# Block-diagonal 128x128 operands for the batched triangular inverses of an RWKV-7 recurrence: three engines share the masking anew

## The reference, cut to what matters

```python
def step(S, inp):
    r_t, w_t, k_t, v_t, kk_t, kka_t = inp
    sa = jnp.einsum('bhvk,bhk->bhv', S, kk_t)
    S = (S * w_t[:, :, None, :]
         - sa[..., None] * kka_t[:, :, None, :]
         + v_t[..., None] * k_t[:, :, None, :])
    y_t = jnp.einsum('bhvk,bhk->bhv', S, r_t)
    return S, y_t
```

## Time and profile before

| what | value |
|---|---|
| time, median of 3 runs | 2113.97 us (2113.3 to 2117.39) |
| the profiled execution | 2113.75 us, of which the span is 2112.0 us |
| mean granted TensorE clock | 0.992 |
| busy: TensorE, VectorE, ScalarE, GpSimd | 95%, 67%, 48%, 8% of the span |
| recurrence with its inverses | about 431 us to 830 us after the span's start |

### The profile page before, as it was taken

How to read it: one execution, slowest core, us unless ns; L and a number is a source line. 1 busy time by engine, 2 the same in 40 slices (tenths; PEclk the granted TensorE clock), 3 DMA queues, 4 the chain that set the end, 5 groups by cost and what they waited for, 6 DMA issues and landing times.

```text
span 2112.0 us, 42671 instructions
## 1 busy us (share of the span) xinstructions
PE 2013.4 (95%) x16558; PEld 1629.3 (77%) x16558; DVE 1418.9 (67%) x2272; ACT 1008.1 (48%) x1765; POOL 174.7 (8%) x183
## 2 busy tenths in 40 slices
PE   5999999988888889999999999999999999999998
PEld 4877777777777776788888888888667778888886
DVE  7788888876666664555563655799786776445355
ACT  6666666645656665333232332442665434334243
POOL 5230000000233332200000000000000000000000
PEclk9999999999999999999999999999999999999999
DMA  4445555563333322233333333333113322333332
GB/s 121 122 143 164 168 178 183 178 139 74 94 74 75 89 59 82 80 90 99 99 96 98 95 99 90 100 90 100 50 41 100 100 70 81 99 95 95 100 92 78
DMA packets 395952, 215.19 MB, mean 102 GB/s; under 512 B 85136, under 2 KB 374312, under 8 KB 395816
## 3 DMA queue, kind: packets, MB, share of 16 engines
q1 hardware_dynamic: 395608, 213.18, 35.2%
q10 hardware_dynamic: 208, 0.06, 0.0%
HBM read 181.68 MB, written 31.52 MB: 101 GB/s over the span
## 4 chain that ended last, share of the span: by engine, by line
PE 86%; DVE 6%; ACT 3%; issue 3%; DMA 1%; SPq 1%; POOL 0%; DVEq 0%; ACTq 0%; POOLq 0%
PE bank L1911 23%; PE bank L1913 23%; PE bank L1912 23%; PE bank L596 3%; PE bank L573 1%; PE bank L604 1%; PE bank L506 1%; PE bank L547 1%; PE bank L520 1%; PE bank L1108 1%; PE bank L526 1%; ACT inv L821 1%; PE bank L539 1%; DVE inv L922 1%; PE bank L553 1%
## 5 line engine op out<-in xcount | busy, mean ns | idle before, releaser
L1911 PE MATMUL bank<-xl,w_hi 128*128 128x512 f32 x1568 | 615.7, 393 | 3.9 <-DVE xl L2633 2.5
L1912 PE MATMUL bank<-xl,w_lo 128*128 128x512 f32 x1568 | 611.1, 390 | 0.0
L1913 PE MATMUL bank<-xl,w_hi 128*128 128x512 f32 x1568 | 611.0, 390 | 0.0
L1558 ACT ACTIVATE w_hi<-w_raw 128x1024 fp32r<-128x1024 f32 x278 | 293.1, 1054 | 481.9 <-PE bank L1913 477.4
L2202 DVE TENSOR_TENSOR w_lo<-w_raw,w_hi 128x1024 fp32r<-128x1024 f32 x278 | 342.6, 1232 | 48.7 <-ACT w_hi L1558 40.0
L1911 PEld LDWEIGHTS bank<-xl,w_hi 128*128 128x128 f32 x1568 | 294.5, 188 | 76.6 <-issue 9.9
L1913 PEld LDWEIGHTS bank<-xl,w_hi 128*128 128x128 f32 x1568 | 294.8, 188 | 61.9
L1912 PEld LDWEIGHTS bank<-xl,w_lo 128*128 128x128 f32 x1568 | 294.9, 188 | 60.6 <-issue 0.5
L1911 PE MATMUL bank<-xh,w_hi 128*128 128x512 f32 x448 | 183.0, 409 | 10.9 <-DVE xh L2207 10.7
L1913 PE MATMUL bank<-xh,w_hi 128*128 128x512 f32 x448 | 175.5, 392 | 0.0
L1912 PE MATMUL bank<-xh,w_lo 128*128 128x512 f32 x448 | 175.4, 392 | 0.0
(11 more groups left out here) (385 smaller groups left out, 3165.5 us busy)
## 6 DMA issues: line engine op xcount, KB each, us to landing
w_raw<-in_a_w_in SPq DMA_DIRECT2D x64, 512.0 KB, 4.2
w_raw<-in_b_w_in SPq DMA_DIRECT2D x64, 512.0 KB, 4.1
w_raw<-in_w_ffn_up SPq DMA_DIRECT2D x42, 512.0 KB, 4.0
w_raw<-in_w_in SPq DMA_DIRECT2D x36, 512.0 KB, 3.8
w_raw<-in_a_w_out SPq DMA_DIRECT2D x16, 512.0 KB, 4.2
w_raw<-in_b_w_out SPq DMA_DIRECT2D x16, 512.0 KB, 4.0
w_raw<-in_w_ffn_down SPq DMA_DIRECT2D x16, 512.0 KB, 4.1
d_g<-sq SPq DMA_DIRECT2D x16, 256.0 KB, 2.2
```

The lines of the kernel that those rows point to most:

```text
L1558: A(w_hi[0:rows, slot, 0:nkb, 0:ncol], w_raw[0:rows, slot, 0:nkb, 0:ncol], ACT.Copy).then_inc(s_hi, units)
L1911: mm(outp, wh, xlo, start=start, stop=False)
L1912: mm(outp, wl, xhi, start=False, stop=False)
L1913: return mm(outp, wh, xhi, start=False, stop=stop)
```

## The change

- `nix` now holds +(I + L): GpSimd fills it with identities once, ahead of the recurrence, and VectorE writes only the strict part over it, with predicated copies from the product banks. L910 (times -1, times mask) and L918 (subtract the identity) are gone. The half-precision operand and its low half become block diagonal tiles of 128x128 per chunk, `nixd` and `nixlod`, cleared once by GpSimd. ScalarE fills the two diagonal blocks of `nixd` (`rounded`, two copies for each group, right after `turned_out`), GpSimd those of `nixlod` (`low_part`, two subtractions for each tile).
- TensorE's `newton_v` and `residual` use them: `both_heads` issues one matmul of 128x128 weights for each chunk in place of two of 64x64, and `diagonal` one of 128 partitions in place of two of 64.
- VectorE reads a group's product banks within two steps (`first_steps`, `second_steps`); `masked`, which came a step later, is folded in. The start of the inverse is made from `nix` in single precision.
- The sign: X is now minus the inverse, so that the mask of the start stays as it is, and `recurrence_evac` scales by 1.0 in place of -1.0.

```diff
             def diagonal(n, twice):
-                for hs in rows:
-                    mm(bank[n][hs, 0:4 * C], (two16 if twice else one16)[hs, hs], eyes4[hs], start=True, stop=False,
-                       skip_group_check=True)
+                mm(bank[n][:, 0:4 * C], (two16 if twice else one16)[:], eyes4, start=True, stop=False,
+                   skip_group_check=True)
+
+            def both_heads(n, lhsT, rhs_, stop=True):
+                g = GROUPS[n][1]
+                for c in range(4):
+                    last = mm(bank[n][:, c * C:(c + 1) * C], lhsT[:, 4 * g + c, :], rhs_[:, 4 * g + c, :], start=False,
+                              stop=stop, skip_group_check=True)
+                return last
...
             def newton_v(t, level):
                 for n, (a, g) in enumerate(GROUPS):
+                    if level == 1:
+                        pe.wait_ge(R["nix16_made"], 8 * t + 2 * n + 2)
                     inverse_ready(t, level - 1, n)
                     diagonal(n, True)
-                    each(n, 0, nix16[a], inv2[a][:, 0], start=False).then_inc(R["v_summed"], 1)
+                    both_heads(n, nixd[a], inv2[a][:, 0]).then_inc(R["v_summed"], 1)
...
             def residual(t):
-                    pe.wait_ge(R["low_made"], 2 * t + a + 1)
+                    pe.wait_ge(R["low_made"], 4 * t + 2 * a + 2)
...
-                    each(n, 0, nixlo16[a], inv2[a][:, 0], start=False, stop=False)
-                    each(n, 0, nix16[a], inv2[a][:, 0], start=False).then_inc(R["e_summed"], 1)
+                    both_heads(n, nixlod[a], inv2[a][:, 0], stop=False)
+                    both_heads(n, nixd[a], inv2[a][:, 0]).then_inc(R["e_summed"], 1)
...
-                scaled(sv[b][hs, :, c, h, :], both(5, 2 * C), -1.0).then_inc(R["u_copied"][h], 1)
+                scaled(sv[b][hs, :, c, h, :], both(5, 2 * C), 1.0).then_inc(R["u_copied"][h], 1)
...
+            def rounded(t, n):
+                a, g = GROUPS[n]
+                cr = slice(4 * g, 4 * g + 4)
+                act.wait_ge(R["nix_made"], 8 * t + 2 * n + 2)
+                if t == 0 and n == 0:
+                    act.wait_ge(s_const, 7)
+                for hs in (slice(0, C), slice(C, P)):
+                    copy(nixd[a][hs, cr, hs], nix[a][hs, cr, :]).then_inc(R["nix16_made"], 1)
...
                             turned_out(t, s // 2)
+                            rounded(t, s // 2)
...
-            def negated(t, n):
-                a, cr, (p0, p1) = group(n)
-                dve.wait_ge(R["products_summed"], 4 * t + n + 1)
-                for hs, p in ((slice(0, C), p0[0:C, :, 0, :]), (slice(C, P), p1[C:P, :, 1, :])):
-                    V.scalar_tensor_tensor(out=nix[a][hs, cr, :], in0=p, scalar=-1.0,
-                                           in1=wide(strict, hs.start, hs.stop, 4), op0=ALU.mult,
-                                           op1=ALU.mult).then_inc(R["nix_made"], 1)
             def first_steps(t, n):
                 a, cr, (p0, p1) = group(n)
+                b = t % 2
+                dve.wait_ge(R["products_summed"], 4 * t + n + 1)
+                if t == 0 and n == 0:
+                    dve.wait_ge(s_const, 5)
+                if t and n < 2:
+                    dve.wait_ge(R["low_made"], LOWS * (2 * t - 1 + n))
+                    dve.wait_ge(R["nix16_made"], LOWS * 4 * t)
+                V.copy_predicated(nix[a][0:C, cr, :], wide(strict.bitcast(I32), 0, C, 4),
+                                  p0[0:C, :, 0, :]).then_inc(R["nix_made"], 1)
+                V.copy_predicated(nix[a][C:P, cr, :], wide(strict.bitcast(I32), C, P, 4),
+                                  p1[C:P, :, 1, :]).then_inc(R["nix_made"], 1)
+                TT(ra[b][:, a, cr, 0, :], p0[:, :, 1, :], wide(incl, 0, P, 4), ALU.mult)
+                TT(st_q[b][C:P, a, cr, 0, :], p0[C:P, :, 0, :], wide(strict, C, P, 4), ALU.mult)
+
+            def second_steps(t, n):
+                a, cr, (p0, p1) = group(n)
+                b = t % 2
+                TT(st_q[b][0:C, a, cr, 2, :], p1[0:C, :, 1, :], wide(strict, 0, C, 4), ALU.mult)
+                TT(ra[b][:, a, cr, 1, :], p1[:, :, 0, :], wide(incl, 0, P, 4), ALU.mult).then_inc(
+                    R["products_masked"], 1)
                 dve.wait_ge(R["nix_made"], 8 * t + 2 * n + 2)
-                TT(nix16[a][:, cr, :], nix[a][:, cr, :], eyes[:, cr, :], ALU.subtract).then_inc(R["nix16_made"], 1)
-                TT(st_q[t % 2][C:P, a, cr, 0, :], p0[C:P, :, 0, :], wide(strict, C, P, 4), ALU.mult)
-                TT(st_q[t % 2][0:C, a, cr, 2, :], p1[0:C, :, 1, :], wide(strict, 0, C, 4), ALU.mult)
-                dve.wait_ge(R["nix16_made"], 4 * t + n + 1)
-                TT(inv2[a][:, 1, cr, :], nix16[a][:, cr, :], bmask[:, 0, :].unsqueeze(1).to_broadcast([P, 4, C]),
+                TT(inv2[a][:, 1, cr, :], nix[a][:, cr, :], bmask[:, 0, :].unsqueeze(1).to_broadcast([P, 4, C]),
                    ALU.mult).then_inc(R["q0_made"], 1)
...
             def low_part(t, a):
-                gp.wait_ge(R["nix16_made"], 4 * t + 3 + a)
-                o(G.tensor_tensor(nix[a][:], nix[a][:], eyes[:], ALU.subtract))
-                G.tensor_tensor(nixlo16[a][:], nix[a][:], nix16[a][:], ALU.subtract).then_inc(R["low_made"], 1)
+                gp.wait_ge(R["nix16_made"], 8 * t + 6 + 2 * a)
+                for h, hs in enumerate((slice(0, C), slice(C, P))):
+                    G.tensor_tensor(nixlod[a][hs, :, hs], nix[a][hs], nixd[a][hs, :, hs], ALU.subtract).then_inc(
+                        R["low_made"], 1)
+                    gp.wait_ge(R["low_made"], 4 * t + 2 * a + h + 1)
...
+            gp.wait_ge(s_unit, U_MIX + 3 * (CI - 1) + 2)
+            for m in nix:
+                gt.tensor_copy(m[:], eyes[:]).then_inc(s_const, 1)
+            for m in nixd:
+                gt.memset(m[:], 0.0).then_inc(s_const, 1)
             gp.wait_ge(s_spill, SPILL_MIX + SPILL_TILE * CI)
+            for m in nixlod:
+                o(gt.memset(m[:], 0.0))
```

More of the change, by code:

```diff
@@ L21 @@
 BF16 = mybir.dt.bfloat16
+I32 = mybir.dt.int32
 ALU = mybir.AluOpType
@@ L248, in program @@
         head_mean = over("head_mean", [P, P])
+        nixd = [over("nixd0", [P, NCH, P], F16)]
         assert spot <= xh_at
@@ L259, in program @@
         nix = [over(f"nix{a}", [P, NCH, C]) for a in range(2)]
-        nix16 = [over(f"nix16_{a}", [P, NCH, C], F16) for a in range(2)]
         inv2 = [over(f"inv2_{a}", [P, 2, NCH, C], F16) for a in range(2)]
+        rhs = over("rhs", [P, 2, C])
         st_pc = [over(f"st_pc{n}", [P, 2, NCH]) for n in range(3)]
-        assert spot <= big_at + 2 * 32768
+        nixd.append(over("nixd1", [P, NCH, P], F16))
+        assert spot <= big_at + 2 * 32768, spot
         spot = big_at + 2 * 32768
@@ L276, in program @@
         tt = [over(f"tt{n}", [P, 2, NCH, C]) for n in range(2)]
-        nixlo16, w16 = ([over(f"{n}_{a}", [P, NCH, C], F16) for a in range(2)] for n in ("nixlo16", "w16"))
-        rhs = over("rhs", [P, 2, C])
+        nixlod = [over(f"nixlod{a}", [P, NCH, P], F16) for a in range(2)]
+        w16 = [over(f"w16_{a}", [P, NCH, C], F16) for a in range(2)]
         yr_a = over("yr_a", [P, T])
@@ L468, in program @@
         PAIRS = CI // 2
+        LOWS = 2
         LOAD_Q, LOAD_BC, LOAD_V, LOAD_ENDS = 16 * 6, 16 * 8, 16 * 6, 16 * 4
@@ L922, in first_steps @@
-                TT(inv2[a][:, 1, cr, :], nix16[a][:, cr, :], bmask[:, 0, :].unsqueeze(1).to_broadcast([P, 4, C]),
-                   ALU.mult).then_inc(R["q0_made"], 1)
-            def masked(t, n):
-                a, cr, (p0, p1) = group(n)
-                TT(ra[t % 2][:, a, cr, 0, :], p0[:, :, 1, :], wide(incl, 0, P, 4), ALU.mult)
-                TT(ra[t % 2][:, a, cr, 1, :], p1[:, :, 0, :], wide(incl, 0, P, 4), ALU.mult).then_inc(
-                    R["products_masked"], 1)
+                b = t % 2
@@ L965, in recurrence_vector @@
                         continue
-                    if s in (2, 4, 6, 8):
-                        masked(t, s // 2 - 1)
                     if s in (0, 2, 4, 6):
-                        negated(t, s // 2)
+                        first_steps(t, s // 2)
                     elif s in (1, 3, 5, 7):
-                        first_steps(t, s // 2)
+                        second_steps(t, s // 2)
                     elif s == 8:
```

## The result

The changed kernel takes 2092.24 us (median of 4 runs, 2087.0 to 2094.74) against 2114.79 us (4 runs, 2113.3 to 2117.39) of the kernel before on the same chip: a ratio of 0.9889, 95% interval 0.987 to 0.9908. The profiled execution took 2093.78 us with a span of 2092.0.

What follows compares the result with a forecast made beforehand. No engine is full in the recurrence, so order and waits decide. Stops -9.8, full-array matmuls +3.4 and front -0.4 sum to -6.8 on 2113.75: 2107.0 us, range 2095 to 2120.

Steps and rivals of the forecast that it cites:

- the stops' term: TensorE's Newton part: fewer instructions mean one instruction-fetch stop less per turn and shorter remaining ones, -9.8 us together.
- the product's pitch: TensorE's V and residual products: 35 ns per full-array matmul of 64 columns, +3.4 us, ends 0 and +9.
- Rival B: TensorE's `both_heads`: full-array weight load not hidden behind 64 columns, so slower, 2123 us; chance 0.12.
- The predicated copies: VectorE's mask writes from the product banks in the front: 421 ns each, taken from a row of the same shape.
- rival D: VectorE's predicated copy takes 842 ns, +0.84 us per group, half on the chain: 2120.6 us; chance 0.06.
- The pair: ScalarE's two added SBUF-to-SBUF copies per group, right behind `turned_out`: 0.77 us.
- the queue behind the fourth pair: ScalarE at the front's end: last group's added copies push later work by 0.77 us; net +0.2 per norm turn.
- transposes that come sooner: Front: group 3's transposes come about 0.5 us sooner, as VectorE no longer holds them.
- Rival A: Front: ScalarE absorbs all four pairs of copies and VectorE's saving counts, -12 us: 2095 us; chance 0.15.
- Rival E: ScalarE in the front: two more pairs of copies not absorbed, 1.5 us in 7 turns: 2118 us; chance 0.07.
- C: Newton part: stops go but ScalarE's L821 copies and the chain's evacuations fill them, no gain: 2113 us; chance 0.15.
- Fills and low parts: GpSimd's fills of `nix` and `nixd` and its `low_part` subtractions: no cost; +2 us if VectorE lacks room.

Runs made afterwards that it cites:

- e1: Changed kernel with TensorE's matmuls put back to 64x64 quarters, masks, roundings and signs as changed: 2115.48 us, ratio 1.0015 to the kernel before.
- e7: Changed kernel with all matmuls in quarters again and diagonals of 512 columns instead of 256, second half thrown away: 2116.38 us.
- e2: Changed kernel plus one-column quarter matmuls ahead of each group in the Newton part, 5 in V and 9 in the residual: 2125.14 us.
- e5: Kernel before with only the diagonal made one full-array matmul, products still in quarters: 2116.94 us, ratio 1.0015.
- e6: Changed kernel with the diagonal in two quarter matmuls again, products kept full-array: 2108.37 us, ratio 0.9975 to the kernel before.
- e3: Changed kernel plus 136 one-column matmuls per turn in the front, 17 ahead of each group's products and transposes: 2109.58 us.
- e9: Changed kernel plus long-fulfilled waits on TensorE, five ahead of each V group and nine ahead of each residual group: 2108.31 us.
- e4: Changed kernel with group 3's two rounded copies written by VectorE in step 9 instead of ScalarE in step 7: 2083.82 us.

## Why the prediction was wrong, point by point

**The step that failed: the stops' term.** I gave -9.8 us for the stops, with an end of -16. Measured: 37.5 to 14.15 us over the recurrence, -23.4; in the Newton part -3.05 us per turn, where I had -1.2. The mechanism was the right one (e1 puts the quarters back and all of the gain is lost), its size was wrong, and by an error of reading. I took a stop as the thing that a packet costs, 0.87 us, and multiplied by the packets saved. But a stop is only what is left over: the time between two packets less the time that the instructions of one last. In the Newton parts the fetches start every 4.13 us in the median before and every 4.26 after, and the six turns hold 7.5 packets each before, 7.0 in e1 and 6.2 after: 29.87 / 7.5 = 3.98, 29.60 / 7.0 = 4.23, 26.18 / 6.2 = 4.2. The change takes 272 instructions out of a turn, 1.06 packets at 256, and 3.4 (against e1) to 3.7 us of the Newton part with them: 3.2 to 3.5 us for one packet. So one packet less is worth most of the whole interval, not the stop that is seen in it, as long as the rest of the work still fits into what remains, and it does: 23.88 us busy. I could have had this from the same trace: the stops come every 4 us, and 24.6 us of work in 29.9 leave 5 us to win before work is the limit. My own ends were drawn from the same wrong unit.

It fits the others. e7 and e1, same count, work 26.93 and 24.91: 29.55 and 29.60 us. e2, e5 and e6 have nearly as much work as the packets take time, or more (29.19, 28.49 and 28.02 us), and last 0.6 to 1.5 us longer than their work. e3 has the added packets in the front; its Newton part holds 6.2 packets a turn as the changed kernel's does, and lasts as long. It does not give the size of e9, whose packets are those of the changed kernel and whose Newton part is 2 us longer. How much of the pace is the fetch and how much the sequencer's handling of each instruction stays open: no run changed the one without the other. The Trainium skill (Runtime: NRT & Kernel Launch, section Instruction fetch mechanics) has the crossing of a block as mostly hidden. The traces agree for the front, where e3's eight more packets added no stop, and not for the Newton part, where nearly all of the 43 stops fall.

**The full-array matmul.** I took 35 ns for the product's pitch, +3.4 us. Measured: L614 0.12 us for four, as eight quarters before, and 0.11 for the diagonal. So the lower end, 0, was right, and with TensorE's busy time in the Newton part 0.7 us lower per turn there is no cost at all. Rival B (2123) is refuted by the same rows; the Trainium skill's 81 ns for a load and matmul of 128 columns (TensorE: Matmul & The Clock Gate, section Back-to-back issue gap) does not carry over to 64 columns, where the trace has 30. What neither B nor I had was the change of shape: with only one of its two halves the change would have lost 3 us (e5) or gained 6 (e6).

**VectorE.** The predicated copies take 0.44 to 0.45, forecast 0.42; rival D's 0.84 is out. L922's successor lost time that I had left it (693 to 428 ns): I had it exposed to GpSimd's norm as before, but with L918 gone it comes at another moment and meets the GpSimd operation that reads one tensor instead of the one that reads two (timelines above).

**ScalarE.** The pair takes 0.83 to 0.85, forecast 0.77. The front of a turn with a norm grew 0.57 us, forecast 0.2; turn 0 gained 1.09 and turn 1 lost 0.91, forecast -0.8 each. In sum +3.3, forecast -0.4. The mechanism is as written, the queue behind the fourth pair; e4 takes that pair off and the front falls by 0.74, nearly the 0.77 that I had for it. What was mis-sized is what I set against it, 0.5 us for transposes that come sooner: without the pair the front of e4 is only 0.17 us shorter than before. The wait at its end moved from VectorE's L760 to ScalarE's L761. Rival A's shorter front did not come; that its 2095 was near the time is luck, for the time came from the stops. Rival E holds in half: no two more pairs, but 0.57.

**C**, that something fills the stops, is refuted: Newton part -3.69 us, and waits for VectorE and ScalarE in it stay at 0.65 us per turn (0.62 before). Fills and low parts cost nothing visible, as forecast.

By the measured terms: stops and work in the Newton part -23.9, front +3.3, together -20.7 against -6.8.

## What to carry to other kernels

When a profile shows regular issue stops in a stretch of small matmuls, compare the length of the stretch with its busy time, not the stops with zero: if it is paced by its instructions, dropping instructions pays by most of the interval from packet to packet (here 3.2 to 3.5 us for 256 of them, against 0.87 us of visible stop), down to the busy time, and lengthening those that stay can be free (here for 2 us a turn, e7). Merge quarter-array matmuls into full-array ones for whole runs and not one by one, since each change between the shapes costs (0.1 us here). Work that is moved to another engine counts by what is queued behind it there, not by that engine's busy share: the best version here is the change with its last pair of copies given back to VectorE (2083.8 and 2086.6 us in two series).

## What was not expected of the hardware

- A full-array matmul behind 64x64 ones, and the other way round, costs 0.10 to 0.11 us more: 0.22 for 0.11 and 0.24 for 0.12 in e5, 0.23 and 0.22 in e6. Within one shape the pitch is 15 ns for a quarter and 30 for a full array of 64 columns.
- Nine waits that are long fulfilled cost some 0.23 us of TensorE's time, and five some 0.09, in a dense stretch (e9).
- 16 us more of TensorE's work cost under 1 us (e7 against e1): a stretch in which the array is 84% busy (24.91 of 29.60 us) can still take its length from something else.
- VectorE's mask of two SBUF tensors took 1.51 us beside a GpSimd operation that reads two tensors (before) and 0.41 beside one that reads a single one (after). The type of its first input changed too, and no run separates the two.
